# When zero rows are stored and when the first cached keys are loaded in a hybrid decoder step

## The reference: what is computed

```
def even_mixer(x, pos, past_len, mla_past, swa_past, ...):
    c_q, c_kv, k_r, swa_qkv = split(x @ w_in)
    q = rms_norm(c_q) @ w_uq;  q_lat = q[nope] . w_uk;  q_rope = rope(q[rope])
    kv_all = [mla_past, rows(c_kv, k_r)]
    o_mla = mla_attend(q_lat, q_rope, kv_all) . w_uv
    for g, (win, dil) in enumerate(((128, 1), (512, 4), (2048, 16))):
        prefix = zeros(win) if swa_past is None else swa_past[g]   # prompt: zeros
        kv_g = concatenate([prefix, kv_new])
        new_bufs.append(kv_g[:, -win:])                            # an output
        o, lse = dilated_group_attend(q_g, kv_g, ...)
    return [o_mla, combine(o, lse)] @ w_out, rows, new_bufs
```

## Time and profile before

| | us |
|---|---|
| median of 3 timed runs | 2848.34 |
| lowest and highest | 2845.81, 2850.04 |
| the profiled execution | 2838.72 |
| its span in the trace | 2836.9 |

### The profile page before, as it was taken

One profiled execution on the slowest core, in us unless ns is written; L12 is line 12 of the kernel. 1 busy time (PEld: TensorE's weight loads), 2 busy tenths in 40 slices (PEclk: granted clock), 3 DMA queues, 4 the chain that ended last, 5 costly groups with the idle time before them and its releaser, 6 DMA issues. The chain is left out here.

```text
span 2836.9 us, 40591 instructions
## 1 busy us (share of the span) xinstructions
PE 2623.5 (92%) x16201; PEld 2174.7 (77%) x16201; DVE 1442.9 (51%) x3440; ACT 351.4 (12%) x1020; POOL 673.5 (24%) x678
## 2 busy tenths in 40 slices
PE   7879996689899999999999999888999999999997
PEld 4555363344559999999999967454899999999997
DVE  1431003002238997997555322113599799955553
ACT  2311012001212112110000010011211111100000
POOL 0154200000001332444333100000033244443330
PEclk8899998789999999999999999999999999999999
DMA  4697978988561998999999998569169999999995
GB/s 143 220 370 239 316 253 303 408 333 295 239 251 56 389 390 293 352 372 337 409 409 409 343 338 311 196 226 399 64 254 379 339 329 343 347 399 409 409 409 197
DMA packets 249865, 885.13 MB, mean 312 GB/s; under 512 B 31802, under 2 KB 39130, under 8 KB 238879
## 3 DMA queue, kind: packets, MB, share of 16 engines
q1 hardware_dynamic: 165630, 591.13, 56.0%
q0 software_dynamic: 84048, 291.41, 27.1%
HBM read 863.08 MB, written 109.08 MB: 343 GB/s over the span
## 5 line engine op out<-in xcount | busy, mean ns | idle before, releaser
L2652 PE MATMUL ps<-xT,front 128*128 128x192 f32 x4096 | 686.0, 326 | 8.2 <-DMA front<-in_peer_uT 6.8
L2652 PEld LDWEIGHTS ps<-xT,front 128*128 128x128 f32 x4096 | 663.2, 190 | 12.8 <-DMA front<-in_peer_uT 9.9
L2678 PE MATMUL ps<-p1e_S,p_qT 128*128 128x192 f32 x2048 | 337.1, 327 | 6.3 <-DMA p_qT<-in_peer_v 6.3
L2678 PE MATMUL ps<-p0e_S,p_qT 128*128 128x192 f32 x2048 | 336.9, 327 | 4.9 <-DMA p_qT<-in_peer_v 4.9
L2678 PEld LDWEIGHTS ps<-p1e_S,p_qT 128*128 128x128 f32 x2048 | 332.4, 190 | 10.8 <-DMA p_qT<-in_peer_v 10.5
L2678 PEld LDWEIGHTS ps<-p0e_S,p_qT 128*128 128x128 f32 x2048 | 332.4, 190 | 9.1 <-DMA p_qT<-in_peer_v 9.0
L2430 DVE CUSTOM_DVE_ANT_0 front<-front,x_tok 128x1024 f32<-128x1024 f32 x256 | 309.9, 1219 | 7.6 <-DMA front<-in_peer_u,p0e_expert 2.7
L2331 POOL DMA_INDIRECT front<-in_peer_u,p0e_expert x128 | 153.1, 1196 | 387.4 <-DVE p0e_dots L2430 206.0
L2331 POOL DMA_INDIRECT front<-in_peer_u,p1e_expert x128 | 153.1, 1196 | 386.5 <-DVE p1e_dots L2430 204.8
L2441 DVE SCALAR_TENSOR_TENSOR h_tok<-front,p1e_dots,h_tok 128x1024 f32<-128x1024 f32 x127 | 163.1, 1285 | 141.5 <-DMA front<-in_peer_v,p1e_expert 140.7
L2441 DVE SCALAR_TENSOR_TENSOR h_tok<-front,p0e_dots,h_tok 128x1024 f32<-128x1024 f32 x127 | 163.2, 1285 | 141.5 <-DMA front<-in_peer_v,p0e_expert 140.6
(11 more groups left out here) (480 smaller groups left out, 3077.4 us busy)
## 6 DMA issues: line engine op xcount, KB each, us to landing
front<-in_peer_uT SPq DMA_DIRECT2D x256, 512.0 KB, 6.9
p_qT<-in_peer_v SPq DMA_DIRECT2D x256, 512.0 KB, 7.3
out_swa_sample<-in_cache_swa_w SPq DMA_DIRECT2D x32, 2040.0 KB, 22.1
e_ring<-in_swa_kT SPq DMA_DIRECT2D x16, 1024.0 KB, 9.0
e_arena<-in_swa_v SPq DMA_DIRECT2D x16, 1024.0 KB, 13.8
out_swa_sample<-in_cache_swa_w SPq DMA_DIRECT2D x8, 2016.0 KB, 31.5
e_ring<-in_mla_pages SPq DMA_DIRECT2D x56, 272.0 KB, 4.9
e_ring<-in_attn_w_in SPq DMA_DIRECT2D x6, 2048.0 KB, 37.2
```

The source lines that it names most:

```text
L2652: mm = pe.matmul(k.ps[:, SB[i % len(SB)], 0:TD], ur[:, i % NU, c, :], k.xT[:, c, D0:T], start=(c == 0), stop=(c == KC - 1))
L2678: mm = pe.matmul(k.ps[:, c // 2, c % 2 * TD:(c % 2 + 1) * TD], vr[:, i % NV, c * P:(c + 1) * P], S[:, i, :], start=False, stop=(i == STEPS ...
```

## The change

The 16 zero-row stores are issued by SP in the query stage, behind the 8 copies that stood there already, and no longer in the prompt's latent attention behind the pages. The first four key pieces of the samples' window attention are asked for in the turning stage, ahead of SP's wait for the bias tables, and no longer in the prompt's window attention behind the window stores. No instruction is added or removed.

```diff
@@ query_stage, block.sync @@
             sp.dma_start(e["mask"][:, :, :], io["causal"]).then_inc(mask_landed, 16)
-            k.copy_some(sp, 8)
+            k.copy_some(sp, 24)
             sp.wait_ge(mask_landed, 16)
@@ BiasByDistance.sync @@
         self.first_loads(sp)
-        k.copy_some(sp, 16)
@@ even_mixer @@
+                def keys_and_tables(sp):
+                    preload_window_keys(k, sp, room)
+                    sp.wait_ge(k.bias_tabled, BiasTables.count)
+
                 turn_stage(k, "kturn", [
...
-                    lambda sp: sp.wait_ge(k.bias_tabled, BiasTables.count))
+                    keys_and_tables)
...
                 attend_prompt(k, "swp", units, 3 * SEQ, 1.0, SWA_SCALE, Stores(
                     lambda sp: store_windows(k, kv, sp), k.window_stored, 16 * N_WINDOW_STORES,
-                    lambda sp: preload_window_keys(k, sp, room), queries.gpsimd), e["ring"][:, 0:4608])
+                    None, queries.gpsimd), e["ring"][:, 0:4608])
```

## The result

| | before, us | after, us |
|---|---|---|
| median of 5 timed runs each, in turn on one chip | 2845.81 | 2826.80 |
| lowest and highest | 2844.71, 2850.04 | 2820.95, 2831.09 |
| the profiled execution | 2838.72 | 2831.09 |
| its span | 2836.9 | 2829.3 |
| ratio after to before | | 0.9930 (0.9912 to 0.9947) |

What follows compares the result with a forecast made beforehand. SP's zero-row issue was taken to hold the gap before the samples' latent attention, and key transfers the samples' window attention. 16.0 + 3.5 + 3.0 = 22.5 us off 2848.34 gave 2826 us, range 2818 to 2837.

Steps and rivals of the forecast that it cites:

- zero rows, the gap they leave: Between prompt's and samples' latent attention: without SP's zero stores the samples' stage starts at about 134.7, not 150.7; 16.0 us.
- zero rows, where they go: Query stage: zeros written by about 81 us, SP done at about 77, 6 us before the last compute; cost 0.
- zero rows, inside the samples' stage: Samples' latent attention: faster clock at the start and shorter page wait, at most 4.6 us, at least 0; taken 3.5.
- first keys, net: Samples' window attention 4.2 us ahead, less about 1.2 for late window stores; 3.0 us net, between -0.1 and 4.2.
- the third rival: The change doesn't do what it says: GpSimd's bias rows or something unseen also holds the gap; 0 to 5 us, chance 0.06.
- A second step: Before the samples' latent attention: the last page, asked for at about 125, lands 4.9 us later, by 130.
- the cover of 1 to 5 us: Before the samples' latent attention: margin by which pages land, or DMA engines empty, ahead of the start at about 134.7.
- The check by bytes: Pages, gathers and bias rows, 10.9 MB: 8.6 moved by 128 us, 2.3 left at 400 GB/s, engines empty by 134.
- The page wait at the third unit: Samples' latent attention: TensorE's 2.82 us wait for pages behind the zeros' tail would fall to under 1 us.
- The clock's 1.8 us: Start of samples' latent attention: TensorE stands about 1 us, not 16, so its first products run at full clock; 1.8 us.
- The 1.2 us that I took off for late stores: Prompt's window attention: SP standing behind keys, half of a 6.4 us slip, closes the stage 0.6 + 0.5 us late.
- the slow first eight stores of before: Prompt's window attention: 6.01 us against 2.81 for the last eight, taken as a sign that SP can be stopped.

Runs made afterwards that it cites:

- e6: Kernel after, with the four key pieces asked for in the prompt's window attention, ahead of its 59 stores; 2826.34 us, ratio to before 0.9927.
- e2: Kernel before with only the key pieces moved to the turning stage, zero rows left in the prompt's latent attention; 2840.33 us, ratio 0.9985.
- e5: Kernel after, with GpSimd's three bias-row stores reshaped (128 rows slowest) and issued at the end of the samples' latent attention; 2819.80 us, ratio to before 0.9900.
- e3: Kernel after, with GpSimd's three bias-row stores written with the 128 rows, not the 4 heads, as slowest dimension; 2822.11 us, ratio to before 0.9922.
- e4: Kernel after, with the three bias-row stores in their old shape issued by SP behind the pages, not by GpSimd; 2843.29 us, ratio to before 0.9992.
- e1: Kernel before with only the zero rows moved to the query stage, key pieces left behind the window stores; 2834.26 us, ratio 0.9962.
- e7: Kernel after run once more, nothing altered, on the chip of e5 and e6; 2827.61 us, ratio to before 0.9929.

## Why the prediction was right and where it was wrong

By its own steps, from the profiles:

| term | forecast, us | measured, us |
|---|---|---|
| zero rows, the gap they leave | 16.0 | 11.1 |
| zero rows, where they go | 0 | 0 |
| zero rows, inside the samples' stage | 3.5 | 0.7 |
| first keys, net | 3.0 | 3.4 |
| sum | 22.5 | 15.2 |

**The gap: the step that failed.** "So the sample stage starts at about 134.7 instead of 150.7": I let the block close with the last of SP's issue and VectorE's compute, and took GpSimd to be done with its last issue at 117.93. It is done when its last transfer has landed. In five traces the block opens 0.6 us behind that landing (141.3 and 141.91; 138.9 and 139.55; 136.3 and 136.94; 140.5 and 141.14 in e6; 140.5 and 141.12), and in all seven that have these stores in this block GpSimd's DRAIN ends 0.4 us behind it, also in before and e2, where SP's zeros came last. In e5, with the stores out of the block, it opens 0.30 us behind VectorE. Of 16.0 us 11.1 were gained, and e5 gains nearly all of the other 4.9 (gap 0.5 us). The rows could have been seen before the result: the trace of before has the landing at 144.4, so once the zeros go they are next in line. As they stood there they would have left 5 us of gain; without the zeros beside them the last one lands 21.3 us after its issue and not 27.6, which gave the other 6. I named the rows in the third rival ("GpSimd's bias rows ... or something not seen holds the stage too") and gave that 0.06, because the gap ended 0.85 us behind SP's last issue. That shows only who is last, not who is next.

A second step failed with it: "the last one at about 125, with 4.9 us to landing, is there by 130". In after the last page is asked for at 127.3 and lands 13.0 us later, 3.2 us behind VectorE. The 4.9 us is a median over the run, and with the rows in flight the four last pages took 8.3 to 13.0 (7.2 to 12.4 already in before). So the cover of 1 to 5 us was not there, and GpSimd's leaving the block sooner would alone have brought about 1.3 us (e3).

The check by bytes could not see it. It counted 3.1 MB of bias rows as if they ran at the sum of all engines, 400 GB/s. For its first 29 us it was right: from 101.6 to 130.6 us, the same stretch of after, the engines moved 299 GB/s where it had 298. It was the rest that didn't go at 400: the rate fell to 310 GB/s from 134 to 136 and to 106 from 138 to 140, while the last page and the last rows still ran on few engines. From SP the same shape keeps only a quarter of them busy (0.26, 101 GB/s in e4); from GpSimd the three in flight together took half of their time.

**Inside the samples' stage.** The forecast had two parts. The page wait at the third unit fell as said (2.82 us to under 1). The clock's 1.8 us never came, because TensorE stood 5 us instead of 1: the granted clock was 1.00 until 140 and 0.50 from 142. Stage to stage it gives 0.7 us, which is less than the spread among the kernels whose instructions are the same here (103.1 us in after, 106.1 in e1). And e5 shows that the step was wrong in itself: at the full clock from the start the stage is no shorter, 103.3 us. I had written that the clock's gain would be lost in the wait "if the pages come no sooner", and then took a value near the upper end. The lower end, 0, was the right one.

**The zeros' place.** Right in mechanism and cost: DMA share 1.05 from 70 to 84, the stage's length the same (34.7 and 34.8). SP is done at 77.1, but on the clock of before that is 74.5 and not 77, so the equal numbers are chance; the margin is 9.2 us and not 6.

**The keys.** The gross gain was forecast at 4.2 us and is 3.4 from before to after, 4.4 by the means of e2's section. The 1.2 us that I took off for late stores was the mis-sized term, 0 in the trace: SP stands (7.83 us for eight stores), but slips by 1.7 us in the end and not by 3.2. I had read the slow first eight stores of before (6.01 us) as a sign of what keys would add; they were a stand of their own, which went when the new one came. The last store is still 3.7 us ahead of VectorE's end. e6 shows the far side: with a slip of 6.4 us the next stage opens 2.7 us behind VectorE. The four pieces landed 14 us after the first was asked for, not within 12, and the waits for keys fell by 2.8 us, not 4.

**Why the total was close all the same.** The measured terms add up to 15.2 us. From 2848.34 that gives 2833, and the kernel runs at 2826.8 and 2827.6. From the query stage to the next projection the traces even give only 13.2 us (550.1 to 536.9), since 1.7 us go between the samples' latent attention and the window projection and 0.5 behind the last transposes; the second profile, without that 1.7, gives 13.3. The timed gain is 15 to 25 us, and 16.5 to 24 in e7's comparison, so by the one trace of before 5 to 7 us are not placed. For the time, 2.5 us come from the median of before, which was 2845.81 in the new runs. For the gain, the trace of before itself is the likely cause, though with one such trace this isn't shown. Its execution was faster than every timed one. Behind the next projection, where nothing was changed, it takes 2237.5 us, and the two of after 2240.6 and 2240.8. And e2 and after, which differ by the zero rows alone, are 12.9 us apart by their traces over the same distance and 13.5 by their medians (taken at different times): there the two ways agree. The zeros alone (10.8 us, 7.1 to 14.8) and the keys alone (4.3, 1.7 to 6.8) agree with their stages, and their sum, 15.1, lies at the lower end of the interval for both. So the hit on 2826 is partly luck: two terms were too large by 7.7 us together, one too small by 0.4, and what the traces do not place made up for most of it.

The prediction has some slips that change nothing in this: it was the fourth zero row, not the third, that took 4.86 us to issue; the lower end of 19.5 us is not the sum of its terms' lower ends (15.9); and the range's lower end is 2819.5 by its own terms, not 2818.

## What to carry to other kernels

When something is taken off the end of a stage, list for every engine when it is free to leave, and read the second latest: that is the new bound, as long as the thing taken away didn't slow it. Then do the same for what the next stage's first instruction waits for. For an engine that issues its own transfers count to their landing until the trace shows otherwise, and read the time to landing from the transfers issued at that place, not from a median over the run. A faster clock in front of a stream that sets the pace brought nothing here; opening the whole stage earlier, its loads included, did. Empty DMA time beside compute, as in the query stage, was a free place for stores that nobody waits for.

## What the runs showed of the hardware that I had not expected

- At the end of this block GpSimd waits in its DRAIN until its own direct stores have landed: 0.4 us from landing to the DRAIN's end in seven traces, and 0.6 us to the opening in the five where it comes last, whatever the landing was (136.3 to 146.5 us). In after the next two ends of blocks with transfers of GpSimd's own show it too: the DRAIN ends 2.2 us behind the last gather's landing (226.6 us) and 0.9 us behind that of the bias tables (349.3 us). SP's takes 0.1 to 0.5 us and leaves its transfers moving: the block opens 0.75 us behind its last issue in e4, and in after its DRAIN is over at 127.8 with the last page landing at 140.3.
- Issued by SP, three stores of 1 MB whose slowest dimension is 4 keep 4 of 16 DMA engines busy (share 0.26, 101 GB/s), take SP 14.3 us to issue, and hold up what SP asks for next by 19.8 us. A store of 1 MB from GpSimd beside pages took up to 21.3 us to land, and the four pages beside it 8.3 to 13.0 us where 3.2 to 4.7 is usual (after, e5). Issued by GpSimd, the same three left SP's issue of pages where it was (ended at 127.65 us in after, 128.24 in e4).
- 8.4 MB of zero rows written beside full TensorE work moved at 402 to 405 GB/s (70 to 76 and 76 to 84 us of after), no slower than the 401 in the standstill.
